# Feed-forward stages: each high weight tile meets both parts of the rows in one product of 512 columns; pooling: group products ahead of the norm

## The reference

```python
def swiglu_2(xn, wg, wu, wd):
    return (jax.nn.silu(xn @ wg) * (xn @ wu)) @ wd

def pool_mixer(xn, w_grp, b, scale):
    ...
    cs = jnp.pad(jnp.cumsum(xf, axis=1), ((0, 0), (1, 0), (0, 0)))
    for g, w in enumerate(POOL_WINDOWS):          # windows 2, 4, 8, 16
        ...
        mean = (jnp.take(c, hi, axis=1) - jnp.take(c, lo, axis=1)) / (hi - lo).astype(f32)[:, None]
        outs.append(mean - xf[..., g * POOL_GROUP:(g + 1) * POOL_GROUP])
    ...
    y = jnp.einsum('blgc,gcd->blgd', d, w_grp).reshape(B, L, D) + b
    return y * scale
```

## Time and profile before

| | us |
|---|---|
| median of 3 runs | 3132.03 |
| the profiled execution | 3133.39 |
| its span, first to last instruction | 3131.6 |
| TensorE busy in it | 2977.8 (95%) |
| VectorE busy | 2068.8 (66%) |
| ScalarE busy | 1628.9 (52%) |
| chain of work that ended last: PE, DVE, ACT | 86%, 6%, 5% |
| mean granted TensorE clock | 0.971 |

### The profile page before, as it was taken

The page is one execution under the profiler, slowest core; times in us unless marked ns, Lnnn a source line. Parts: engine busy times, 40 slices in busy tenths (PEclk is TensorE's granted clock), DMA queues, the critical chain, the costliest instruction groups (busy, mean ns, idle before and its releaser), DMA issues.

```text
span 3131.6 us, 46969 instructions
## 1 busy us (share of the span) xinstructions
PE 2977.8 (95%) x20320; PEld 2729.0 (87%) x20320; DVE 2068.8 (66%) x1930; ACT 1628.9 (52%) x1604; POOL 260.6 (8%) x201
## 2 busy tenths in 40 slices
PE   7999999999979999999999999999599889999999
PEld 7998999999878888888787587999499889877999
DVE  5786565578648888888788565554555465565553
ACT  5446444544547767767676452445354344353442
POOL 1130110023000000000000201100001001012010
PEclk9999999999979999999999899999699999999999
DMA  6444555544429999989899041556055545522453
GB/s 199 157 145 138 161 178 175 176 151 145 148 103 371 349 348 375 352 339 352 337 377 337 18 159 42 183 171 225 13 159 176 171 150 180 168 95 68 131 176 125
DMA packets 358820, 612.63 MB, mean 196 GB/s; under 512 B 11375, under 2 KB 323397, under 8 KB 323664
## 3 DMA queue, kind: packets, MB, share of 16 engines
...
...
## 4 chain that ended last, share of the span: by engine, by line
PE 86%; DVE 6%; ACT 5%; issue 2%; DMA 1%; ACTq 0%; DVEq 0%
PE ps L326 16%; PE ps L327 16%; PE ps L328 16%; PE ps L1162 5%; PE ps L1164 5%; PE ps L1163 5%; PE ps L1143 2%; PE ps L1141 2%; PE ps L1142 2%; PE ps L1641 2%; PE ps L627 2%; PE ps L1656 2%; ACT whi L259 2%; DVE wlo L270 1%; PE ps L1611 1%
## 5 line engine op out<-in xcount | busy, mean ns | idle before, releaser
L270 DVE TENSOR_TENSOR wlo<-raw,whi 128x2048 fp32r<-128x2048 f32 (+1 forms) x573 | 1315.3, 2301 | 640.1 <-ACT whi L259 636.0
L259 ACT ACTIVATE whi<-raw 128x2048 fp32r<-128x2048 f32 (+1 forms) x573 | 1083.6, 1894 | 273.1 <-PE ps L328 140.8
L326 PE MATMUL ps<-HX,whi 128*128 128x256 f32 x1824 | 528.4, 290 | 42.6 <-DVE HX L469 26.5
L327 PE MATMUL ps<-HX,whi 128*128 128x256 f32 x1824 | 522.5, 286 | 0.0
L328 PE MATMUL ps<-HX,wlo 128*128 128x256 f32 x1824 | 522.3, 286 | 0.0
L326 PE MATMUL ps<-HXB,whi 128*128 128x256 f32 x1760 | 500.4, 284 | 0.0
L328 PE MATMUL ps<-HXB,wlo 128*128 128x256 f32 x1760 | 498.1, 283 | 0.0
L327 PE MATMUL ps<-HXB,whi 128*128 128x256 f32 x1760 | 498.1, 283 | 0.0
L326 PEld LDWEIGHTS ps<-HX,whi 128*128 128x128 f32 x1824 | 356.8, 196 | 46.8 <-ACT HX L465 17.9
L327 PEld LDWEIGHTS ps<-HX,whi 128*128 128x128 f32 x1824 | 356.7, 196 | 0.6 <-issue 0.2
L328 PEld LDWEIGHTS ps<-HX,wlo 128*128 128x128 f32 x1824 | 356.5, 195 | 0.0
...
## 6 DMA issues: line engine op xcount, KB each, us to landing
raw<-in_c_experts SPq DMA_DIRECT2D x264, 1024.0 KB, 4.9
raw<-in_w_in SPq DMA_DIRECT2D x72, 1024.0 KB, 5.0
raw<-in_ff_w_gate SPq DMA_DIRECT2D x44, 1024.0 KB, 5.3
raw<-in_ff_w_up SPq DMA_DIRECT2D x44, 1024.0 KB, 5.3
raw<-in_ff_w_down SPq DMA_DIRECT2D x32, 1024.0 KB, 5.1
raw<-in_dense_w SPq DMA_DIRECT2D x30, 1024.0 KB, 5.3
raw<-in_hy_w_in SPq DMA_DIRECT2D x24, 1024.0 KB, 5.2
...
```

The source lines that it names most:

```text
L259: e.activation(m.whi[:, i % NSPLIT, 0:n], m.raw[:, i % NRAW, 0:n], ACT.Copy).then_inc(*k.up("act", "hi", i))
L270: e.tensor_tensor(m.wlo[:, i % NRAW, 0:n], m.raw[:, i % NRAW, 0:n], hi, ALU.subtract).then_inc(*k.up("dve", "lo", i))
L326: e.matmul(o, wh, xh, start=first and t == k0, stop=False)
L327: e.matmul(o, wh, xl, start=False, stop=False)
```

## The change

**Feed-forward.** For each feature tile the high weight tile is multiplied with both parts of the rows in one product: 512 columns, high part to the left half of a bank, low part to the right half. The low weight tile times the high part is added to the right half (256 columns). So each 128-feature column of a panel takes a bank of its own, and its value is left half plus right half. ScalarE copies the right halves into `sil` or `hf` (`act_right_halves`), VectorE adds the left halves (`dve_left_halves`), waits for itself, and then does the product with the row factor, or with the gate, from SBUF. The y sums are added to X in two steps, right half, then left half.

**Pooling.** The group weights are linear, and so are the windows: the products with the weights now come first, with rows times gain (made in ffn2's down panels, without the row factor) as the stationary operand, so that the result has rows on the partitions. The row factor is turned onto the partitions (`pe_factors_down`) and multiplied in on the way out of PSUM (`Z`). Then four fp32 products per group with a constant matrix of window weights (`c_windows`, 1 MB, loaded from ScalarE's queue behind ffn2) replace scan, differences, length and subtraction. Bias and scale: chunk 0 of a group on ScalarE, chunk 1 on VectorE.

```diff
+def pe_both_parts(e, k, o, w, c, x, k0, k1, kx, first=True, final=True, fresh=None):
+
+    i = None
+    for t in range(k0, k1):
+        wh, wl = (v[:, t, c:c + 128] for v in w)
+        if fresh:
+            e.wait_ge(*k.at(*fresh, kx + t))
+        e.matmul(o[:, :], wh, x[:, :, kx + t, :], start=first and t == k0, stop=False)
+        i = e.matmul(o[:, L:2 * L], wl, x[:, 0, kx + t, :], start=False, stop=final and t == k1 - 1)
...
 def pe_ffn(e, k, m, s, last, after=None, sums=True):
     for j in range(11):
-        pe_gemm(e, k, m, s, "a", m.HXB, [j], fresh=None if j else ("hx", last))
-        if j == 0:
-            pe_last_sums(e, k, m, last)
-        pe_gemm(e, k, m, s, "b", m.HXB, [j])
+        for name in ("a", "b"):
+            i = pe_panel(e, k, m)
+            w = weights(m, i, 8, 256)
+            for c in range(2):
+                o = pe_take(e, k, m, name, s, j, c)
+                fresh = ("hx", last) if j == 0 and name == "a" and c == 0 else None
+                pe_both_parts(e, k, o, w, 128 * c, m.HXB, 0, 8, 0, fresh=fresh).then_inc(*k.up("mm", name, s, j, c))
+            k.note("mm", "used", i)
+            if j == 0 and name == "a":
+                pe_last_sums(e, k, m, last)
...
-                mm = pe_weights_still(e, k, o[c][:, 0:L], w, 128 * c, m.HID, 0, k1 - k0, k0, first=k0 == 0, final=k1 == 22)
+                mm = pe_both_parts(e, k, o[c], w, 128 * c, m.HID, 0, k1 - k0, k0, first=k0 == 0, final=k1 == 22)
...
+def act_right_halves(e, k, m, name, s, j, dst):
+    for c in range(2):
+        e.wait_ge(*k.at(name, s, j, c))
+        e.activation(dst[:, c * L:(c + 1) * L], ps(k, m, name, s, j, c)[:, L:2 * L], ACT.Copy).then_inc(*k.up("act", "right", name, s, j, c))
+
+
 def act_ffn(e, k, m, panels, s, last, nxt, after=None, sums=True):
     for j in range(11):
         sil, hf = hidden_parts(m, j)
         act_panel(e, k, m, panels)
         if j == 0:
             act_rstd(e, k, m, last, m.rs[:, :])
-        e.wait_ge(*k.at("free", "g", s, "a", j))
+        if j >= 2:
+            e.wait_ge(*k.at("hf", s, j - 2))
+        act_right_halves(e, k, m, "a", s, j, sil)
+        e.wait_ge(*k.at("gate", s, j))
         e.activation(sil, sil, ACT.Silu).then_inc(*k.up("act", "sil", s, j))
         act_panel(e, k, m, panels)
+        if j >= 2:
+            e.wait_ge(*k.at("hid", s, j - 2))
+        act_right_halves(e, k, m, "b", s, j, hf)
         e.wait_ge(*k.at("hf", s, j))
...
+def dve_left_halves(e, k, m, name, s, j, dst):
+
+    for c in range(2):
+        x = dst[:, c * L:(c + 1) * L]
+        e.wait_ge(*k.at("right", name, s, j, c))
+        e.tensor_tensor(x, x, ps(k, m, name, s, j, c)[:, 0:L], ALU.add).then_inc(*k.up("dve", "free", name, s, j, c))
+    e.wait_ge(*k.own("dve"))
+
+
 def dve_ffn(e, k, m, panels, s, last, nxt, after=None):
     for j in range(11):
         sil, hf = hidden_parts(m, j)
         dve_panel(e, k, m, panels)
-        dve_times_norm(e, k, m, s, last, "a", j, sil)
+        dve_left_halves(e, k, m, "a", s, j, sil)
+        e.wait_ge(*k.at("rstd", last))
+        v = sil.rearrange("p (a n) -> p a n", a=2)
+        e.tensor_tensor(v, v, m.wide_rs, ALU.mult).then_inc(*k.up("dve", "gate", s, j))
         dve_panel(e, k, m, panels)
+        dve_left_halves(e, k, m, "b", s, j, hf)
         e.wait_ge(*k.at("sil normed", s, j))
-        e.wait_ge(*k.at("g", s, "b", j))
-        if j >= 2:
-            e.wait_ge(*k.at("hid", s, j - 2))
-        e.tensor_tensor(hf, sil, ps(k, m, "g", s, "b", j)[:, :], ALU.mult).then_inc(*k.up("dve", "free", "g", s, "b", j))
-        k.note("dve", "hf", s, j)
+        e.tensor_tensor(hf, sil, hf, ALU.mult).then_inc(*k.up("dve", "hf", s, j))
         e.wait_ge(*k.at("hidh", s, j))
...
-            e.tensor_tensor(m.X[:, c, :], m.X[:, c, :], ps(k, m, "y", s, c)[:, 0:L], ALU.add).then_inc(
+            o = ps(k, m, "y", s, c)
+            e.tensor_tensor(m.X[:, c, :], m.X[:, c, :], o[:, L:2 * L], ALU.add).then_inc(*k.up("dve"))
+            e.wait_ge(*k.own("dve"))
+            e.tensor_tensor(m.X[:, c, :], m.X[:, c, :], o[:, 0:L], ALU.add).then_inc(*k.up("dve", "free", "y", s, c))
...
 def pe_pooling(e, k, m, s, last):
-    pe_sums(e, k, m, last, 6, 2)
-    k.release("sum", last)
     n = pe_panel(e, k, m)
+    wh, wl = weights(m, n, 8, 256)
+    for g in range(4):
+        o = pe_take(e, k, m, "g", s, "in", g)
+        for j in range(2):
+            oj = o[:, j * 256:j * 256 + 256]
+            for t in range(2 * g, 2 * g + 2):
+                if j == 0:
+                    e.wait_ge(*k.at("hx", last, t))
+                xh, xl = (m.HX[:, p, t, j * 128:j * 128 + 128] for p in range(2))
+                e.matmul(oj, xh, wh[:, t, :], start=t == 2 * g, stop=False)
+                e.matmul(oj, xh, wl[:, t, :], start=False, stop=False)
+                mm = e.matmul(oj, xl, wh[:, t, :], start=False, stop=t == 2 * g + 1)
+        mm.then_inc(*k.up("mm", "g", s, "in", g))
+    k.note("mm", "used", n)
+    pe_last_sums(e, k, m, last)
+    pe_factors_down(e, k, m, s, last)
     pe_hold(e, k, m, "sum", s)
+    Z, A = pool_views(m)
+    e.wait_ge(*k.at("windows"))
     for g in range(4):
-        w = [v[:, 2 * g:2 * g + 2, :] for v in weights(m, n, 8, 256)]
         o = pe_take(e, k, m, "g", s, "out", g)
-        pe_weights_still(e, k, o[:, 0:L], w, 0, m.HX, 0, 2, 2 * g, fresh=("px", s))
-        pe_weights_still(e, k, o[:, L:2 * L], w, 128, m.HX, 0, 2, 2 * g).then_inc(*k.up("mm", "g", s, "out", g))
-    k.note("mm", "used", n)
-    for g in range(3):
-        pe_sums(e, k, m, s, 2 * g, 2)
+        e.wait_ge(*k.at("z", s, g))
+        for i in range(2):
+            ch = 2 * g + i
+            for j in range(2):
+                mm = e.matmul(o[:, i * L:(i + 1) * L], Z[:, j, ch * 128:ch * 128 + 128], A[:, j, g, :], start=j == 0, stop=j == 1)
+        mm.then_inc(*k.up("mm", "g", s, "out", g))
+        if g >= 2:
+            pe_sums(e, k, m, s, 2 * g - 4, 2)
+    pe_sums(e, k, m, s, 4, 2)
...
+def act_windows_in(e, k, m, a, last):
+    e.wait_ge(*k.at("x", last, 0))
+    e.dma_start(m.buf(4), a["c_windows"]).then_inc(*k.land("misc_in", "windows"))
...
     act_panel(e, k, m, panels)
+    act_rstd(e, k, m, last, m.rs[:, :])
+    act_factors_down(e, k, m, s)
+    e.wait_ge(*k.own("act"))
+    for g in (0, 2):
+        o = ps(k, m, "g", s, "in", g)
+        for j in range(2):
+            e.activation(Z[:, j, 256 * g:256 * g + 256], o[:, j * 256:j * 256 + 256], ACT.Copy, scale=m.rst[:, j:j + 1]).then_inc(
+                *k.up("act", "free", "g", s, "in", g))
+        k.note("act", "z", s, g)
+    for g in range(5):
+        if g < 4:
+            c = 2 * g
+            e.wait_ge(*k.at("g", s, "out", g))
+            e.wait_ge(*k.at("shift", s))
+            e.activation(m.buf8(1)[:, c, :], ps(k, m, "g", s, "out", g)[:, 0:L], ACT.Identity, bias=m.buf(5)[:, c:c + 1],
+                         scale=m.col("pl_scale_2", c)).then_inc(*k.up("act", "y", s, g))
+        if g:
+            act_ahead(e, k, m, s, 2 * g - 2, 2, nxt)
...
+    e.wait_ge(*k.at("free", "down", s))
+    for g in (1, 3):
+        o = ps(k, m, "g", s, "in", g)
+        for j in range(2):
+            e.tensor_scalar(Z[:, j, 256 * g:256 * g + 256], o[:, j * 256:j * 256 + 256], m.rst[:, j:j + 1], None, ALU.mult).then_inc(
+                *k.up("dve", "free", "g", s, "in", g))
+        k.note("dve", "z", s, g)
     for g in range(4):
+        c = 2 * g + 1
+        y = m.buf8(1)
         e.wait_ge(*k.at("g", s, "out", g))
-        o = ps(k, m, "g", s, "out", g)
-        for c in (2 * g, 2 * g + 1):
-            e.tensor_scalar(m.buf8(1)[:, c, :], o[:, (c % 2) * L:(c % 2) * L + L], m.col("pl_b_2", c), m.col("pl_scale_2", c),
-                            ALU.add, ALU.mult).then_inc(*k.up("dve", "free", "g", s, "out", g))
+        e.wait_ge(*k.at("y", s, g))
+        e.tensor_scalar(y[:, c, :], ps(k, m, "g", s, "out", g)[:, L:2 * L], m.col("pl_b_2", c), m.col("pl_scale_2", c),
+                        ALU.add, ALU.mult).then_inc(*k.up("dve", "free", "g", s, "out", g))
...
-    act_ffn(e, k, m, panels, "ffn2", "attn", None)
+    act_ffn(e, k, m, panels, "ffn2", "attn", before_mixer(m, "norm_mix_2", 2))
+    act_windows_in(e, k, m, a, "ffn2")
...
+        windows[:, i] = np.where((u >= lo) & (u < hi), 1.0 / (hi - lo), 0.0) - (u == t)
```

More of the change, by code:

```diff
@@ L2227, in dve_pooling @@
-def dve_pooling(e, k, m, panels, s, last, gain, nxt):
-    H = m.buf8(7)
-    for c in range(T8):
-        dve_scale(e, k, m, last, c, H, m.buf(3)[:, 0:L], gain)
-    inv = m.buf(4)[:, 0:1024].rearrange("p (g n) -> p g n", g=4)
-    one, cs, O = m.buf(3)[:, 512:512 + L], pool_sums(m), m.buf8(0)
-    e.wait_ge(*k.at("edges zero", s))
-    e.wait_ge(*k.own("dve"))
-    for c in range(8):
-        e.tensor_tensor_scan(cs[:, c, R + 1:R + 1 + L], one, H[:, c, :], 0.0, ALU.mult, ALU.add).then_inc(*k.up("dve", "scan", s, c))
-    e.wait_ge(*k.at("inv"))
-    for step in range(6):
-        if step < 4:
```

(50 more changed lines are left out.)

20 lines of the change are left out of this document (3 added, 17 removed).

## The result

| | before | changed |
|---|---|---|
| median, us | 3132.45 (3128.88 to 3136.97, 11 runs) | 3140.72 (3134.52 to 3146.8, 11 runs) |
| profiled execution, us | 3133.39 | 3136.85 |
| its span, mean granted clock | 3131.6, 0.971 | 3135.0, 0.972 |

Ratio 1.0028, 95% interval 1.0018 to 1.0037: slower by 0.3%. The forecast was 3128, a gain of 4 us; what came is a loss of 8.3. The measured time lies inside the stated range, 12.7 above the forecast. Part by part the signs were right: the feed-forward stages lose and the pooling gains. Both sizes were off.

A forecast was written before the change was run, and what follows sets the result against it. In feed-forward, TensorE bounds the kernel before, and the ScalarE-VectorE ring after the change; pooling is a VectorE and ScalarE chain. Feed-forward +12.8 and pooling -17 sum to -4.2 us: 3128 from the median 3132.03, range 3113 to 3144.

The forecast's parts named there:

- the ring's size: Gate and up loop of ScalarE and VectorE: two adds lengthen each panel's round by 0.78 to 6.18 us; TensorE needs 5.55.
- the place of the stalls: TensorE waits for low parts from about panel 17 of each stage, and for hidden rows before the third down panel.
- TensorE is 1.8 us later there ... The stage ends level: ffn1's third down panel starts at 141.1, before 139.3; the remaining down products then gain 1.9 us.
- Four products of fp32, 0.22 each as 64 in 13.81: Pooling's window products cost 0.22 us each, or twice that at half clock; first window sums at 11.1 to 12.0.
- The product's saving: Feed-forward products: 512 plus 256 columns replace three of 256, saving 13.3 ns per triple, at most 35.2 us over 2640.
- The ends: Stage ends: adding each y in two dependent steps costs 0.6 us for ffn0, ffn1 and ffn3, 0.5 for ffn4.
- (2): Gate-up loop: each add waits in full, 0.92 instead of 0.78 us, +14 us, giving 3142; chance 20%.
- half-turns: One panel's round through ScalarE and VectorE in the gate-up loop: 5.4 us before, 6.18 forecast after the change.
- (1): Gate-up loop isn't the bound, its adds hide: 35.2 less 3 and 17 are gained, -49 us, giving 3083; chance 5%.
- (3): Wide product isn't cheaper: the 160 uncovered triples of each stage gain nothing, +10.7 us, giving 3139; chance 12%.
- (4): Pooling gains only 14 us, giving 3131; counted within the forecast, no chance of its own.
- The slower case: Whole kernel above 3138.3 us, by a costlier loop, half of the dearer wide product and some mishap; chance 0.22.

The follow-up runs named there:

- fill_stall: Changed kernel, with TensorE doing four product pairs twice in each stage's first down panel, ahead of the wait for the last hidden rows: 3133.84 us, ratio 1.0006.
- no_copies: Changed kernel without ScalarE's copies of right halves in ffn1 to ffn4, VectorE's adds reading X instead: 3141.04 us, ratio 1.0026.
- down_only: Changed kernel with gate and up products as before; wide products stay in the down panels, pooling stays changed: 3109.39 us.
- pool_only: Kernel before with only the pooling part of the change, feed-forward stages as before: 3119.67 us, ratio 0.9959.
- after_again: The changed kernel itself, unaltered, run again beside the version with added products: 3139.35 us, ratio 1.0022.
- the ring opened by hand: Changed kernel with ScalarE making the up panel's high part ahead of its wait for the norm: 3086.37 us, ratio 0.985.

## Why the prediction was wrong, point by point

- **What bounds it, the ring's size, the place of the stalls: right.** 6.18 forecast, 6.19 measured; third down panel at 141.1 forecast, 141.4 measured. Without the slow stretch ffn1 would be at 195.7-1.7=194.0 (fill_stall has 194.3), with 193.5 forecast. ffn0: 10.2 forecast without its end, 10.9 measured. It has two waits of 4.3 us in its gate-up part, each with a slow stretch behind it; since the sum comes out nearly right they seem to cost little. That is argued, not shown; it fits a TensorE that is ahead of the ring and would wait again.
- **"TensorE is 1.8 us later there ... The stage ends level": the step that failed.** A wait behind a late engine was priced at its length alone. Behind 7 of 16 such waits a stretch at half clock cost 1.7 more, where TensorE has no slack. In the profile that is 3.4 us, and shortening the waits gave 5.5 in the medians. The forecast had looked at the clock in the pooling's gap and not asked it of the stalls it made itself. This is the largest piece of the miss.
- **"Four products of fp32, 0.22 each as 64 in 13.81": mis-sized.** The 64 of the earlier trace rows are records, two to a product: 0.43. The two row sums at 0.5 have the same error. The pooling's gap fell by 13.3 (13.6 in the runs' medians), not by 17, and a little less than the lower bound of 14: +3.4. The price isn't all of it. The half clock, which the forecast kept as a bound of 0.9 us on the first group, lies over the first two groups and costs them 1.7. And the forecast let the feed-forward start two groups behind the first; on ScalarE the third group's high parts stand behind the fourth group's bias and scale, which waits 1.18 for its products (2527.72). How the 3.4 divide among these isn't shown. That the clock counts is: no_copies and down_only have 6.8 us at half clock there, and gaps of 25.2 and 25.0.
- **The product's saving: right in ffn1, too high elsewhere.** 13.3 ns were taken everywhere; the down products of down_only gave 9.9, and ffn3's pairs stand at 353 ns.
- **The ends.** I put +2.3 on the five ends. No run isolates them. The gaps outside the pooling moved by -1.8, -0.7, +2.7, -0.9 and +0.4 in the profiles, of which not all is theirs: the one ahead of ffn2 is 148.1 in before and 149.2 in pool_only, whose code there is the same.
- **Rest.** ffn3 is +0.8 and the others +0.4 to +0.7 above the forecast. ffn3's wider pairs are part of that; the rest isn't traced.
- Sum: 3128 + 3.4 (pooling) + 5.5 (the waits' clock, by fill_stall) leaves 2.4 of after_again's 3139.35 for all the rest, and 3.8 of the first 3140.72.
- **The rivals.** (2), "the ring costs more", gave 3142, near what was measured, by a mechanism that isn't there: it needed half-turns above 6.29. (1) had its half-turns of 5.55 only with the ring opened by hand. (3) is refuted by 346 to 353 ns, (4) came true, slightly worse than its 14, and was counted within the forecast. The slower case was given 0.22: a case "waits halve the clock behind them" was missing from the list.

By the figure of the Trainium skill (TensorE: Matmul & The Clock Gate, "Wait — 56ns, not 53.3ns?"), about 2.5 ns per product, an estimate for the wide product's gain is 2.5 ns a triple. The traces don't agree: they show 13 to 14 ns in ffn1, 9.9 in down_only's down products and 7 in ffn3.
